# Turning block 0 of the rows inside the feed-forward ahead of each second mixer, and projecting it first

## The reference

```python
n1 = modulate(rms_norm_2(h, norm_g[l, 0]), sh1, sc1)
h = h + 0.5 * g1[:, None, :] * swiglu_2(n1, ffn_wg[l, 0], ffn_wu[l, 0], ffn_wd[l, 0])

n2 = modulate(rms_norm_2(h, norm_g[l, 1]), sh2, sc2)
y = token_mixing(n2, ang_r, ang_c, lam_init, w_in[l], qk_g[l], lam_p[l], subln_g[l],
                 w_ba[l], w_bb[l], w_gate[l], b_gate[l], w_o[l])
h = h + g2[:, None, :] * y

n3 = modulate(rms_norm_2(h, norm_g[l, 2]), sh3, sc3)
h = h + 0.5 * g3[:, None, :] * swiglu_2(n3, ffn_wg[l, 1], ffn_wu[l, 1], ffn_wd[l, 1])
```

## Time and profile before

| | us |
|---|---|
| median of 3 runs | 3022.71 |
| lowest, highest | 3019.93, 3024.22 |
| the profiled execution, its own time | 3018.76 |
| its span | 3016.1 |
| TensorE busy | 2888.1 (96%) |
| VectorE busy | 1241.2 (41%) |
| ScalarE busy | 420.6 (14%) |
| GpSimd busy | 152.7 (5%) |
| mean granted clock of TensorE, share of full | 0.977 |

### The profile page before, as it was taken

One profiled execution on the slowest core, in us unless ns is written; L12 is line 12 of the kernel. 1 busy time (PEld: TensorE's weight loads), 2 busy tenths in 40 slices (PEclk: granted clock), 3 DMA queues, 4 the chain that ended last, 5 costly groups with the idle time before them and its releaser, 6 DMA issues.

```text
span 3016.1 us, 40818 instructions
## 1 busy us (share of the span) xinstructions
PE 2888.1 (96%) x17886; PEld 1795.8 (60%) x17886; DVE 1241.2 (41%) x2259; ACT 420.6 (14%) x1055; POOL 152.7 (5%) x221
## 2 busy tenths in 40 slices
PE   7799999799999999999998999999999999989998
PEld 5567776543333333333333877586887877577876
DVE  4747775731000000000101676153676776152544
ACT  4430003430000000000000100131101101131100
POOL 6200004200000000000000000000000000000000
PEclk9889999889999999999999999999999999999999
DMA  6237864217999999999998575413774874413542
GB/s 224 86 112 254 276 226 157 107 56 277 380 367 392 358 372 382 376 384 356 376 387 307 206 262 176 173 65 113 256 267 161 282 268 168 147 56 126 162 163 88
DMA packets 266316, 704.99 MB, mean 234 GB/s; under 512 B 9286, under 2 KB 132439, under 8 KB 241556
## 3 DMA queue, kind: packets, MB, share of 16 engines
q1 hardware_dynamic: 225072, 622.39, 56.3%
q10 hardware_dynamic: 38036, 75.61, 7.1%
q0 software_dynamic: 3024, 4.31, 0.5%
HBM read 698.07 MB, written 1.05 MB: 232 GB/s over the span
## 4 chain that ended last, share of the span: by engine, by line
PE 88%; DVE 8%; ACT 2%; DMA 2%; issue 1%; DVEq 0%; POOL 0%; SPq 0%; ACTq 0%
PE PS L1941 85%; DVE PS L1439 1%; DMA ring<-in_w_in_dram 1%; PE PS L2378 1%; DMA ring<-in_moe_w_up_dram 1%; PE PS L2208 0%; DVE SM L1566 0%; PE PS L1977 0%; DVE SM L1823 0%; DVE GS L1492 0%; ACT R L1097 0%; PE PS L2586 0%; DVE PS L1820 0%; DVE R L1414 0%; DVE R L1417 0%
## 5 line engine op out<-in xcount | busy, mean ns | idle before, releaser
L1941 PE MATMUL PS<-ring,R 128*32 128x256 f32 (+2 forms) x3616 | 711.2, 489 | 0.6 <-ACT R L985 0.6
L1941 PEld LDWEIGHTS PS<-ring,R 128*32 128x32 f32 (+2 forms) x3616 | 287.1, 137 | 385.4 <-issue 354.1
L1941 PE MATMUL PS<-XT,ring 128*128 128x128 f32 (+1 forms) x2624 | 396.3, 309 | 9.7 <-ACT GS L1077 7.9
L1941 PEld LDWEIGHTS PS<-XT,ring 128*128 128x128 f32 x2624 | 364.5, 194 | 61.0 <-issue 31.0
L1941 PE MATMUL PS<-ring,GS 128*64 128x384 f32 (+4 forms) x2176 | 305.2, 527 | 0.8 <-ACT XT L1005 0.8
L1941 PE MATMUL PS<-ring,KZ 128*64 128x512 f32 (+3 forms) x2048 | 301.9, 543 | 0.6 <-DMA ring<-in_moe_w_up_dram 0.6
L1941 PEld LDWEIGHTS PS<-ring,GS 128*32 128x32 f32 (+1 forms) x2176 | 103.3, 122 | 197.4 <-issue 192.4
L1941 PEld LDWEIGHTS PS<-ring,KZ 128*64 128x64 f32 (+1 forms) x2048 | 99.5, 123 | 197.1 <-issue 190.5
L1941 PE MATMUL PS<-R,ring 128*128 128x128 f32 x1856 | 216.7, 275 | 0.0
L1941 PEld LDWEIGHTS PS<-R,ring 128*128 128x128 f32 x1856 | 211.9, 192 | 0.0
L1712 DVE TENSOR_TENSOR QT<-QT,PS 128x1536 f32<-128x1536 f32 (+1 forms) x16 | 24.9, 1554 | 439.0 <-PE PS L1941 439.0
(11 more groups left out here) (351 smaller groups left out, 2721.8 us busy)
## 6 DMA issues: line engine op xcount, KB each, us to landing
ring<-in_moe_w_gate_dram SPq DMA_DIRECT2D x32, 2048.0 KB, 11.2
ring<-in_moe_w_up_dram SPq DMA_DIRECT2D x32, 2048.0 KB, 11.0
ring<-in_moe_w_down_dram SPq DMA_DIRECT2D x32, 2048.0 KB, 10.8
ring<-in_moe_w_gate_dram SPq DMA_DIRECT2D x32, 1536.0 KB, 11.2
ring<-in_moe_w_up_dram SPq DMA_DIRECT2D x32, 1536.0 KB, 6.9
ring<-in_moe_w_down_dram SPq DMA_DIRECT2D x32, 1536.0 KB, 8.9
ring<-in_ffn_wg_dram SPq DMA_DIRECT2D x44, 1024.0 KB, 5.5
ring<-in_ffn_wu_dram SPq DMA_DIRECT2D x44, 1024.0 KB, 8.5
```

The lines of the kernel that those rows point to most:

```text
L1941: return e.matmul(o, lhsT, rhs, start=first, stop=last)
```

## The change

Stages 5 and 8 start as a feed-forward does. Block 0's transposes stand between the 14th and the 15th down product of the stage ahead, in banks 1 and 2; ScalarE writes all eight chunks of block 0 there. VectorE makes the gains ahead of its residual adds. The mixer then has the order `PROJ2`: slab 0 and slab 1 of block 0, then block 1's transposes (banks 4 and 5), the gate rows (banks 6 and 7 in place of 4 and 5), then slab 0 and 1 of block 1, and from slab 2 on block 0 and block 1 in turn. `PBANK2` gives the banks. Block 1's chunks are written four by ScalarE and four by VectorE (`turned`, taken out of `ffn`). A slab is given back when its projection of block 1 is done. `mod_of` gives the same numbers as before and new ones for stages 5 and 8; `turn_mod` is gone. A function of the expert stage is renamed (left out here).

```diff
@@ -248,6 +248,9 @@
         SQS = (M2[:, 0:640], M2[:, 2048:2688])
         HBIAS = SM[:, 448:464]
         NLAM = SM[:, 146:147]
+
+        PROJ2 = ((0, 0), (1, 0), (0, 1), (1, 1), (2, 0), (2, 1), (3, 0), (3, 1), (4, 0), (4, 1))
+        PBANK2 = (0, 3, 1, 2, 0, 3, 1, 2, 0, 3)
         GROUPS2 = [("diff", b, hp) for b in range(2) for hp in range(2)]
         GROUPS2 += [("gqa", b, v) for b in range(2) for v in range(2)]
         MX = QT
@@ -298,7 +301,7 @@
         s_x = signal("s_x", mix1=4, ffn1=4, ffn2=4, mix2=4)
         s_sq, s_rstd, s_xsa, s_xsv = sem("s_sq"), sem("s_rstd"), sem("s_xsa"), sem("s_xsv")
         s_xtp = signal("s_xtp", mix1=4, ffn1=4, moe=4, ffn2=4, mix2=4)
-        s_xta = signal("s_xta", mix1=4, ffn1=12, moe=4, ffn2=12, mix2=4)
+        s_xta = signal("s_xta", mix1=4, ffn1=12, moe=4, ffn2=12, mix2=12)
         s_xtv = signal("s_xtv", mix1=4, ffn1=4, moe=4, ffn2=4, mix2=4)
         s_scale = signal("s_scale", ffn2=1, mix2=1)
         s_gbt = signal("s_gbt", ffn2=2, mix2=2)
@@ -480,7 +483,7 @@
 
         def plan_mix2(st):
             for f in range(5):
-                rg.plan(("win", st, f), s_pj(st, 2 * f + 2))
+                rg.plan(("win", st, f), s_pj(st, PROJ2.index((f, 1)) + 1))
             for q in range(2):
                 for ab in range(2):
                     rg.plan(("gate", st, q, ab), s_ga(st, 8 * q + 7 + ab))
@@ -521,7 +524,7 @@
 
         def mod_of(st):
 
-            return (0, 0) if st == 4 else (0, 2) if st == 6 else (1, 0) if st == 7 else (1, 2)
+            return divmod(st - 4, 3)
 
         def gain_of(st, c):
             return vcol("ffn_norm_g", 0, c) if st == 1 else SM[:, 8 + c:9 + c]
@@ -758,7 +761,7 @@
                         e.wait_ge(*s_x(st, 2 * b + h + 1))
                         square(b, h)
                     scale(st + 1, b)
-                    if b == 0 and STAGES[(st + 1) % 10] in ("ffn1", "ffn2"):
+                    if b == 0 and st + 1 < len(STAGES) and STAGES[st + 1] in ("ffn1", "ffn2", "mix2"):
                         turned(st + 1, 0, range(8))
 
             def turned(st, b, chunks):
@@ -786,10 +789,6 @@
                                          bias=shift(c)).then_inc(s_xta.sem, 1)
                         else:
                             e.activation(XT[:, c, :], src, ACT.Copy, scale=gain(c)).then_inc(s_xta.sem, 1)
-
-            def turn_mod(st, l, k):
-                e.wait_ge(*s_scale(st, 1))
-                turn(st, lambda c: SM[:, 8 + c:9 + c], lambda c: MODC[:, l, 24 * k + c:24 * k + c + 1])
 
             def gate_rows(st, B):
 
@@ -1042,12 +1041,14 @@
                 e.wait_ge(s_oadd, 32)
 
             def mix2(st, l):
-                turn_mod(st, l, 1)
-                gate_rows(st, 4)
-                for i in range(5):
-                    c1 = min(512, 2304 - 512 * i)
-                    e.wait_ge(*s_pj(st, 2 * i + 1))
-                    e.activation(PR[:, 512 * i:512 * i + c1], PS[:, 2 * (i % 2), 0:c1], ACT.Copy).then_inc(s_pja.sem, 1)
+                for n, (i, b) in enumerate(PROJ2):
+                    if n == 2:
+                        turned(st, 1, (0, 1, 4, 5))
+                        gate_rows(st, 6)
+                    if b == 0:
+                        c1 = min(512, 2304 - 512 * i)
+                        e.wait_ge(*s_pj(st, n + 1))
+                        e.activation(PR[:, 512 * i:512 * i + c1], PS[:, PBANK2[n], 0:c1], ACT.Copy).then_inc(s_pja.sem, 1)
                 e.wait_ge(*s_lamr(st, 1))
                 e.activation(SM[:, 144:146], SM[:, 144:146], ACT.Exp).then_inc(s_lame.sem, 1)
 
@@ -1203,10 +1204,17 @@
                 e.scalar_tensor_tensor(out=SM[:, 8:16], in0=MODC[:, l, 24 * k + 8:24 * k + 16], scalar=1.0,
                                        in1=VC[:, 0, row:row + 8], op0=ADD, op1=MUL).then_inc(s_scale.sem, 1)
 
-            def turn_mod(st, l, k):
-                gains(st, l, k)
-                e.wait_ge(*s_scale(st, 1))
-                turn(st, lambda c: SM[:, 8 + c:9 + c], lambda c: MODC[:, l, 24 * k + c:24 * k + c + 1])
+            def turned(st):
+
+                for c in (2, 3, 6, 7):
+                    if c == 2:
+                        e.wait_ge(*s_xtp(st, 4))
+                    dst = XT[:, c, P:2 * P]
+                    if st == 1:
+                        e.tensor_scalar(dst, turn_bank(st, 1, c), gain_of(st, c), None, MUL).then_inc(s_xtv.sem, 1)
+                    else:
+                        e.tensor_scalar(dst, turn_bank(st, 1, c), gain_of(st, c), shift_of(st, c), MUL,
+                                        ADD).then_inc(s_xtv.sem, 1)
 
             def t_sum(st, j, n):
 
@@ -1270,15 +1278,7 @@
                         e.tensor_tensor(MODC[:, l, at], col[:, 4 * lo - 16 * b:4 * hi - 16 * b], bias, ADD).then_inc(s_aout, 1)
 
             def ffn(st, F, finish):
-                for c in (2, 3, 6, 7):
-                    if c == 2:
-                        e.wait_ge(*s_xtp(st, 4))
-                    dst = XT[:, c, P:2 * P]
-                    if st == 1:
-                        e.tensor_scalar(dst, turn_bank(st, 1, c), gain_of(st, c), None, MUL).then_inc(s_xtv.sem, 1)
-                    else:
-                        e.tensor_scalar(dst, turn_bank(st, 1, c), gain_of(st, c), shift_of(st, c), MUL,
-                                        ADD).then_inc(s_xtv.sem, 1)
+                turned(st)
                 a11, a21, a12, a22 = (XT[:, 4 * k:4 * k + 4, b * P:b * P + P] for k in range(2) for b in range(2))
                 e.wait_ge(*s_xta(st, 12))
                 e.wait_ge(*s_xtv(st, 4))
@@ -1327,8 +1327,10 @@
                         ada_out(ADA_OUT[st, j])
                     if (st, j) in ADA_SUM:
                         ada_sum(ADA_SUM[st, j])
-                if STAGES[(st + 1) % 10] == "ffn2":
+                if st + 1 < len(STAGES) and STAGES[st + 1] == "ffn2":
                     ahead(st + 1)
+                elif st + 1 < len(STAGES) and STAGES[st + 1] == "mix2":
+                    gains(st + 1, *mod_of(st + 1))
                 for b in range(2):
                     for h in range(2):
                         e.wait_ge(*s_y(st, 2 * b + h + 1))
@@ -1760,11 +1762,12 @@
 
             def mix2(st, l):
                 lam_init = 0.8 - 0.6 * float(np.exp(-0.3 * l))
-                turn_mod(st, l, 1)
-                for i in range(5):
-                    c1 = min(512, 2304 - 512 * i)
-                    e.wait_ge(*s_pj(st, 2 * i + 2))
-                    e.tensor_copy(PR[:, 2304 + 512 * i:2304 + 512 * i + c1], PS[:, 1 + 2 * (i % 2), 0:c1]).then_inc(s_pjv.sem, 1)
+                turned(st)
+                for n, (i, b) in enumerate(PROJ2):
+                    if b == 1:
+                        c1 = min(512, 2304 - 512 * i)
+                        e.wait_ge(*s_pj(st, n + 1))
+                        e.tensor_copy(PR[:, 2304 + 512 * i:2304 + 512 * i + c1], PS[:, PBANK2[n], 0:c1]).then_inc(s_pjv.sem, 1)
 
                 lp = LP[:, l, :].rearrange("p (a d) -> p a d", d=64)
                 lt, lv = SM[:, 16:144].rearrange("p (a d) -> p a d", d=64), SM[:, 144:146]
@@ -2094,7 +2097,7 @@
                     down(last, 0, h).then_inc(s_y.sem, 1)
                 for h in range(2):
                     for f in range(last - 3, last + 1):
-                        if h == 1 and f == last - 1 and STAGES[(st + 1) % 10] == "ffn2":
+                        if h == 1 and f == last - 1 and st + 1 < len(STAGES) and STAGES[st + 1] in ("ffn2", "mix2"):
                             turn_block(st + 1, 0)
                         w = down(f, 1, h)
                     w.then_inc(s_y.sem, 1)
@@ -2491,23 +2494,28 @@
                     e.wait_ge(s_oadd, 2 * it + 2)
 
             def mix2(st, l):
-                turn(st, gate_rows(st, l, 5))
-                for i in range(5):
+                for n, (i, b) in enumerate(PROJ2):
                     c1 = min(512, 2304 - 512 * i)
                     key = ("win", st, i)
                     wt = rg.view(key, 8, c1)
-                    e.wait_ge(*rg.landed[key])
-                    for b in range(2):
-                        if i >= 2:
-                            e.wait_ge(*(s_pjv if b else s_pja)(st, i - 1))
-                        elif i == 0 and b == 1:
-                            e.wait_ge(*s_xtv(st, 4))
-                            e.wait_ge(*s_xta(st, 4))
-                        for c in range(8):
-                            if i == 0 and b == 0:
-                                xt_ready(st, c)
-                            w = mm(PS[:, (2 * i + b) % 4, 0:c1], XT[:, c, b * P:b * P + P], wt[:, c, :], c == 0, c == 7)
-                        w.then_inc(s_pj.sem, 1)
+                    if b == 0:
+                        e.wait_ge(*rg.landed[key])
+                    if n == 1:
+                        e.wait_ge(*s_xta(st, 8))
+                    elif n == 2:
+                        turn_block(st, 1)
+                        gate_rows(st, l, 5, 6)()
```

(17 more changed lines are left out.)

## The result

| | before | changed |
|---|---|---|
| median of 6 runs, us | 3021.47 | 3007.88 |
| lowest, highest | 3019.55, 3024.22 | 3003.99, 3010.76 |
| profiled execution, its own time | 3018.76 | 3006.72 |
| its span | 3016.1 | 3004.9 |
| mean granted clock | 0.977 | 0.979 |

The ratio of the times is **0.9954, with a 95% interval of 0.9941 to 0.9967**: faster by 13.6 us by the medians, where 8.6 were forecast. The direction held, the size didn't; the rest of this document is mostly about the 4 to 5 us that the forecast had not seen.

A forecast was written before the change was run, and what follows sets the result against it. TensorE, busy 96% of the span, was taken as the bound, so only its gaps or lower clock count. Waits of 2 x 3.46 plus 1.70 us of clock give 8.6 us: 3022.71 to 3014.1 us, range 3009.6 to 3019.2.

The forecast's parts named there:

- waits at the two starts: Between downs and projections at both second mixers, 6.99 us shrinks to 3.53 us of work, gaining 3.46 us each.
- Points 1 to 4: Possible waits before block 0's transposes, first projection, block 1's transposes and third projection at each mixer; all taken as 0.
- Both margins of 0.1 us: Time in hand before block 0's transposes and before the third projection at each mixer, some 0.1 us each.
- the outer ends (0.45 and 0.61): Other ends for waits, in us: 0.45 before block 0's transposes, 0.61 before the third projection; 0 was taken.
- the argument on ScalarE's split: ScalarE's smaller, more numerous activations add 2.7 us per mixer, under matmuls; if all in line, gain 0.8 us, not 3.46.
- The clock term: Low-clock stretch (0.58) behind the gap goes: 1.70 us at the second mixer, 0 at the first.
- B: At both mixers the small margins fail, losing 0.45 and 0.61 us; gain 6.5 us, time 3016.2 us; chance 0.15.
- E: Nothing changes because a slab lands only when the old order would have used it; 3022.7 us; chance 0.04.
- D: Late block 0 delays the last two downs; slower from 4.3 us lateness per mixer; chance 0.03.
- C: Clock takes some back: the 1.70 us not gained, one or two more low places; 3015.8 to 3019.2 us; chance 0.20.
- The range's low end: Forecast plus one more low stretch avoided (1.7 us) and the fastest run's 2.8 us below the median: 3009.6 us.
- Theory U: Something reaches beyond the mixer starts whichever mixer is changed; changing each alone adds up to some 5 us over the whole.

The follow-up runs named there:

- the first experiment: No edit: the kernel before and the changed kernel each run again; 3021.01 us (ratio 0.9994) and 3008.47 us (ratio 0.9959) against the kernel before.
- null_act: Kernel before plus eight one-element ScalarE activations per second mixer, where ScalarE idles; 3017.24 us, ratio 0.9993.
- the two single changes: Kernel before with only stage 5 or only stage 8 changed: 3012.82 us (ratio 0.9971) and 3013.72 us (ratio 0.9967).

## Why the forecast was too small

The sum of what the runs show, beside the sum on record:

| term | forecast | from the runs |
|---|---|---|
| waits at the two starts | 2 x 3.46 = 6.9 | 2 x 3.51 = 7.0 |
| clock behind the gap and behind the 2.65 us wait | 1.7 | 2.6 |
| ahead of stage 5 | 0 | 1.3 |
| found in no trace | | 1.5 |
| all | 8.6 | 12.4 |

The last line is the distance between the means of 94 runs of the kernel before (those beside the experiments, and the first experiment) and 17 of the changed one. The chips differ by up to 3.6 us in the mean of the kernel before, so it is not exact; by the first two sets alone it is 13.9.

The granted clock that stands on record for these runs is a second measure, which does not hang on a few traces. (1 - granted clock) x span is on average 69.2 us for the kernel before and 64.0 for the changed one, **5.2 us** less (give or take 1.7); what is left of the time falls by **7.2 us** (give or take 0.9), which is the two waits. A low clock beside idle time is counted in it too, and each clock is on record to 0.001, 3 us, so this holds for means alone. By it the waits of the forecast were right, and nearly all that it lacked is clock, of the mixers' starts and of the rest of the program together.

**Points 1 to 4 held.** No wait before block 0's transposes, none before the first projection, none before block 1's, none before the third projection. Both margins of 0.1 us held too, and the outer ends (0.45 and 0.61) are refuted: VectorE finished 0.2 us ahead of the third projection. The eight chunks took 2.90 us again and the four 1.50, so the rows behind the argument on ScalarE's split carried over unchanged; the added activations lie beside matmuls. That turning ahead alone gains nothing and the projections pay was shown by taking the projections away.

**The clock term was mis-sized.** This is the step that failed. It read: 1.70 at the second mixer, 0 at the first, "which had none". It took one execution for the kernel, and it looked at one place. A low stretch behind a gap is an event with a frequency. Over all traces of mixers with the old start (12 of them) it stands behind the 2.49 us gap in 6: at stage 8 in 4 of 6, for 1.7 us each, and at stage 5 in 2 of 6, for about 1.0 us each in time. Over the 12 with the new start, it stands in none. That makes 4/6 x 1.7 + 2/6 x 1.0 = 1.5 us per kernel, so the term for the gap itself was right by luck of the trace. What was missing is the second place: behind the 2.65 us wait of the earlier trace rows the stretch of 1.65 us stands in 4 of the 6 stages 8 with the old start, the same four that have it behind the gap, and in none of the stages 5, nor in any of the 12 mixers with the new start: another 1.1 us. With so few traces these frequencies are rough. That the one goes with the other was seen in counts; filling the gap in the kernel before took both away, in one trace. By the clocks of all runs the term is 5.2 in place of 1.7. The two traces of the kernel before are of executions 2.9 and 1.2 us below the mean of their own runs, so low stretches that others have may be missing in them; where the rest of the 5.2 us lies was not found.

**No term for what lies upstream.** The prediction has no line for the time ahead of stage 5, where the change has no instruction; it took it as nothing without a reason. The traces put the changed kernel 1.3 us ahead there on average, three traces against two, and their ranges overlap. It begins with the 2 us in the first 22 us of the program, grows to 3.2 us by 312 us, where `null_act` has 3.1 us too, and shrinks again. The cause of each step stays open. In the first pair of profiles it shows as 0.94 us.

**The rivals.** B (margins fail) and E (slabs land late) fell. D's mechanism, downs delayed by a late block, didn't occur. C looked at the clock as something that may take back; its argument, that the same wait comes with either level, was the right observation, and its sign was wrong: it fell to the gain's side. The range's low end was made of one more stretch and the scatter of runs. With 5.2 us of clock in place of 1.7 + 1.7 it would just have held the time, which it missed by 1.7 us.

**What stays open:** where the low clock lies that all runs have and no trace shows; what in a program moves its first 22 us, and why the lead shrinks later; and why the two single changes together exceed the whole by 5 to 6 us (with wide intervals), where a common part of 1.3 us is all that the traces show ahead of stage 5. Theory U is borne out in its sum and not explained.

## What to carry to other kernels

When a norm stands between two products on TensorE, look for work of half of the rows that is independent of it and put as much of it between as the norm takes (here one projection of 6.9 us was enough); moving the transposes alone is worth nothing. When a short wait can't be closed, and the clock falls behind it in the traces, repeat some harmless product in it: 1.7 us of repeats per mixer gave back 3.4 us of slow matmuls. Before a gain of a few tenths of a per cent is credited to an edit, take the trace of the old kernel twice and compare marks upstream of the edit, with an edit that does nothing beside it. The recorded clocks of all runs, averaged, split a gain into waits and clock where two or three traces can't.

## What the runs showed of the hardware

- Waits of TensorE as short as 1.90 and 1.14 us, close together, were followed by the granted clock of 0.60 for 8.5 us, 3.4 us lost, in the changed kernel at both mixers; a single wait of 2.49 us by 1.7 us lost in 6 of 12 cases, and one of 5.15 us by 1.8 and 3.4 us in one trace.
- Where the wait that follows is not yet over, a low clock costs less than it takes: of 1.7 us behind the gap at stage 5, 0.6 us took the place of a wait.
- Filling a gap with 2.68 us of repeats made the kernel 4 to 5 us faster, though no start was earlier by its dependencies; the granted clock of the runs accounts for 4.6 us.
- In the trace of a program whose only edit runs some 1900 us later, the transfers of the first 22 us were faster (284 and 388 GB/s for 186 and 248) and TensorE's work at 95 us came 2 us earlier; at stage 5 it was 0.5 us earlier than the mean of the two traces without the edit.
